# Expert gates added into a zeroed DRAM array by indirect transfers instead of routing matmuls

## The chip, the cores and the metric

One Trainium2 chip, one core. The time is device microseconds of one execution; where several were made, their median.

## The reference

One layer of a decoder, 512 tokens of 2048 numbers, all in float32. What comes ahead (projections, convolution branch, differential attention, first layer norm) is not touched. The change lies in the layer of experts ("peer"), for each block of tokens:

```python
q = (xb @ w_q).reshape(TOKEN_BLOCK, PEER_HEADS, 2, PEER_HALF)
s = jnp.einsum('thcd,hcnd->thcn', q, sub_keys).astype(jnp.float32)
vals, idx = lax.top_k(s, PEER_TOPK)
cand = vals[:, :, 0, :, None] + vals[:, :, 1, None, :]
cand_ids = idx[:, :, 0, :, None] * PEER_N_KEYS + idx[:, :, 1, None, :]
best, pos = lax.top_k(cand.reshape(TOKEN_BLOCK, PEER_HEADS, PEER_TOPK * PEER_TOPK), PEER_TOPK)
...
g = jax.nn.softmax(best, axis=-1)
h = jax.nn.gelu(jnp.einsum('td,thkd->thk', xb, u_tab[ids]))
return jnp.einsum('thk,thkd->td', g * h, v_tab[ids])
```

Each token picks 8 x 16 = 128 of 128 x 128 = 16384 experts, each with a gate g. The expert's down row u gives one number h, and g * h weighs its row v.

## The kernel before

A matmul in float32 accuracy is made of three float32r passes (lines 631 to 633): the weights raw, loaded from ws in units of 1 MB (two blocks of 128 x 1024), are split into whi (ACT, line 1027) and wlo = raw - whi (POOL, line 594, or DVE, line 1611), the activations likewise into ahi and alo. one_block issues 24 matmuls. Loads are issued by SP (load_unit, line 415), each as soon as the wlo of the unit two earlier is done.

Stages: projections and heads (B1), branches (B2), output projection and residual (B3, the result is res, kept in SBUF), the experts' queries and key scores (B4), then two long stages: up-projection of all 16384 experts (256 blocks from B5; 64 expert_steps of 4), and value stage (256 blocks from B6). For the first TU = 352 tokens both are done densely: all experts, 352 columns. The remaining 160 tokens go sparsely: POOL gathers the picked rows (gather_rows, line 614: an indirect DMA of 128 rows of 8 KB), and DVE multiplies and sums each with the token (dot, line 1623, a scalar_tensor_tensor of 128 x 2048). 32 of the tokens (x1e, extra_dot) are spread over 128 partitions, 32 gathers; the last 128 take 128 gathers: NUP = 160 in all, with RING = 4 in flight. DVE names the next row (line 1617) when a buffer is free, and then does its other work in program order: lo_part, dot, and in some blocks one-hots.

For the dense tokens the up-projection gives gelu(x u) of every expert, which ACT writes from PSUM to DRAM (gelu_spill, [128 units, 128, 384]). The value stage needs it times the gate of (expert, token), zero where a token did not pick the expert. This array of gates is built by matmul, while the up-projection runs: for each token, PE multiplies two one-hot matrices,

```python
mm = pe.matmul(ps_g[s][:, k * P:(k + 1) * P], hot1[:, s, k], hot2w[:, s, k],
               start=True, stop=True)
```

hot1[pick, i1] and hot2w[pick, i2] times the gate, contracted over the token's 128 picks. 384 tokens (352 and the 32 extra ones, whose "gate" is g * h and whose gelu is set to 1) are done 4 at a time: DVE makes the one-hots (one_hots, line 1600), ACT scales them (scale_hots, line 1204), PE multiplies (route, line 875), ACT copies the result to gst (take_group, line 1211). A tile is RT = 64 tokens in 32 blocks; the first 16 blocks carry a group each. SP stores gst (4 MB) to route_spill per tile (line 500), six tiles in all. gst has the place of res, so res is stored before (spill_x1, line 475) and loaded back at the end of the up-projection (line 532). In the value stage load_hg loads gelu and gates for two units, and DVE multiplies them (expert_weights, line 1698).

Before the first tile PE transposes the picks (turn_picks, line 865) and DVE copies them from PSUM (line 1590).

The order of POOL in this stretch: the subtractions of the first 40 blocks of the up-projection, spread_picks, then 160 gathers and 128 gathers of v rows, with nothing between. From block 40 (DVE_LO) on, DVE subtracts.

## Time and profile before

| | |
|---|---|
| median of 3 runs | 3902.03 us (3900.24 to 3908.92) |
| the profiled execution | 3903.89 us, span 3902.1 us |
| PE matmul busy | 3808.9 us, 98% |
| DVE busy | 2682.2 us, 69% |
| ACT busy | 1403.7 us, 36% |
| POOL busy | 1265.6 us, 32% |
| read from HBM, written | 788.21 MB, 67.11 MB |

PE is TensorE's matmul queue, PEld its weight loads, DVE VectorE, ACT ScalarE, POOL GpSimd, SP the queue that issues most loads. The view of lines gives a group's busy time and the mean of one; the timeline gives each instruction's start and length and, in brackets, the idle time before it and what ended it; windows add up busy time between two points. Busy time of PE counts overlapping matmuls once, so it says that the engine has work, not that it runs at its peak. For gathers POOL's time is that of issuing, and the landing is listed apart.

### The profile page before, as it was taken

The page shows a single profiled execution, that of the slowest core. Times are in us where ns is not written, and L with a number is a line of the kernel's source. Part 1 is how long each engine was busy: PE and PEld are TensorE (multiplying, and loading weights), DVE is VectorE, ACT ScalarE, POOL GpSimd, SP SyncE. Part 2 cuts the span into 40 slices and gives each one's busy share as a digit, 9 for nine tenths or more (in the row PEclk, how much of TensorE's full clock was granted, in tenths as well). Part 3 has the DMA queues.
Part 4 walks back from the last instruction along what each step waited for, and adds up shares of the span by engine and source line. Part 5 has one row for each costly group of instructions (what it writes and reads, how often), then busy time and mean ns, then how long its engine had stood idle before and what let it go on. Part 6 is the DMA issues. An engine that isn't in the chain of part 4 may idle for free.

```text
span 3902.1 us, 57973 instructions
## 1 busy us (share of the span) xinstructions
PE 3808.9 (98%) x20449; PEld 3471.3 (89%) x20449; DVE 2682.2 (69%) x3814; ACT 1403.7 (36%) x1992; POOL 1265.6 (32%) x620
## 2 busy tenths in 40 slices
PE   8999999999998999999999999989999999999999
PEld 6888888878886889999999999989999999999777
DVE  3555555534413899878878878778888888898642
ACT  4433444441114223446546545222222222222442
POOL 4444444434443447422222222212212211222233
PEclk9999999999999999999999999999999999999999
DMA  4222222224433324698998898978877877787332
GB/s 156 95 97 97 102 94 94 94 99 152 148 121 108 108 89 160 232 367 321 361 373 314 340 378 328 404 294 315 306 288 279 318 289 283 285 311 278 119 105 78
DMA packets 210825, 856.40 MB, mean 219 GB/s; under 512 B 17520, under 2 KB 107824, under 8 KB 119216
## 3 DMA queue, kind: packets, MB, share of 16 engines
q1 hardware_dynamic: 137648, 515.62, 36.6%
q0 software_dynamic: 41600, 302.04, 19.2%
q10 hardware_dynamic: 31488, 37.76, 2.7%
q8 instruction: 30, 0.49, 0.1%
q14 instruction: 59, 0.48, 0.0%
HBM read 788.21 MB, written 67.11 MB: 219 GB/s over the span
## 4 chain that ended last, share of the span: by engine, by line
PE 75%; DVE 9%; DMA 7%; DVEq 3%; ACT 3%; issue 2%; ACTq 1%; SPq 0%
PE bank L631 24%; PE bank L633 23%; PE bank L632 23%; DMA raw<-ws 7%; DVE wlo L1611 2%; PE bank L875 2%; DVEq L1625 2%; DVE yacc L1715 2%; ACT whi L1027 1%; DVE sc L1416 1%; PE bank L674 1%; DVEq L1709 1%; PE bank L693 1%; DVE hot L1600 1%; DVE res L1757 1%
## 5 line engine op out<-in xcount | busy, mean ns | idle before, releaser
L1027 ACT ACTIVATE whi<-raw 128x1024 fp32r<-128x1024 f32 x784 | 820.6, 1057 | 2253.9 <-PE bank L633 1429.2
L631 PE MATMUL bank<-ahi,whi 128*128 128x352 f32 (+1 forms) x3968 | 1434.6, 362 | 32.2 <-DVE alo L1365 7.9
L632 PE MATMUL bank<-alo,whi 128*128 128x352 f32 (+1 forms) x3968 | 1413.8, 356 | 0.0
L633 PE MATMUL bank<-ahi,wlo 128*128 128x352 f32 (+1 forms) x3968 | 1413.6, 356 | 0.0
L594 POOL TENSOR_TENSOR wlo<-raw,whi 128x1024 fp32r<-128x1024 f32 x316 | 792.0, 2510 | 1050.3 <-ACT whi L1027 1021.5
L631 PEld LDWEIGHTS bank<-ahi,whi 128*128 128x128 f32 x3968 | 749.8, 189 | 126.7 <-issue 35.9
L633 PEld LDWEIGHTS bank<-ahi,wlo 128*128 128x128 f32 x3968 | 749.4, 189 | 77.3
L632 PEld LDWEIGHTS bank<-alo,whi 128*128 128x128 f32 x3968 | 749.5, 189 | 72.1 <-issue 0.5
L1611 DVE TENSOR_TENSOR wlo<-raw,whi 128x1024 fp32r<-128x1024 f32 x472 | 574.7, 1223 | 190.6 <-ACT whi L1027 188.3
L631 PE MATMUL bank<-xwhi,whi 128*128 128x384 f32 x2048 | 686.7, 335 | 19.3 <-ACT hst L1226 10.3
L633 PE MATMUL bank<-xwhi,wlo 128*128 128x384 f32 x2048 | 685.7, 335 | 0.0
L632 PE MATMUL bank<-xwlo,whi 128*128 128x384 f32 x2048 | 685.6, 335 | 0.0
L614 POOL DMA_INDIRECT vrows<-v_tab,idxs x128 | 218.3, 1705 | 878.1 <-DVE idxs L1617 868.3
L614 POOL DMA_INDIRECT urows<-u_tab,idxs x160 | 250.7, 1567 | 673.3 <-DVE idxs L1617 663.3
L631 PEld LDWEIGHTS bank<-xwhi,whi 128*128 128x128 f32 x2048 | 385.7, 188 | 21.7 <-issue 21.4
L632 PEld LDWEIGHTS bank<-xwlo,whi 128*128 128x128 f32 x2048 | 385.7, 188 | 0.0
L633 PEld LDWEIGHTS bank<-xwhi,wlo 128*128 128x128 f32 x2048 | 385.6, 188 | 0.0
L1715 DVE SCALAR_TENSOR_TENSOR yacc<-vrows,hd,yacc 128x2048 f32<-128x2048 f32 x127 | 298.7, 2352 | 23.4 <-issue 20.6
L1623 DVE SCALAR_TENSOR_TENSOR urows<-urows,x1n 128x2048 f32<-128x2048 f32 x128 | 292.5, 2285 | 0.0
L1416 DVE SCALAR_TENSOR_TENSOR sc<-glu,cur,sc 128x512 f32<-128x512 f32 x232 | 270.1, 1164 | 17.3
L1204 ACT ACTIVATE hot2w<-hot,gT 128x128 f32<-128x128 f32 x384 | 122.9, 391 | 116.6 <-DVE hot L1600 116.6
L1382 DVE RECIPROCAL rcp<-sums 128x2 f32<-128x2 f32 x32 | 5.3, 166 | 231.1 <-ACTq L1085 231.1
(218 smaller groups left out, 2809.8 us busy)
## 6 DMA issues: line engine op xcount, KB each, us to landing
raw<-ws SPq DMA_DIRECT2D x394, 1024.0 KB, 4.9
gelu_spill<-hst ACTq DMA_DIRECT2D x128, 192.0 KB, 3.7
route_spill<-gst SPq DMA_DIRECT2D x24, 1024.0 KB, 14.8
hg<-gelu_spill SPq DMA_DIRECT2D x64, 384.0 KB, 6.7
hg<-route_spill SPq DMA_DIRECT2D x64, 384.0 KB, 7.4
gate_spill<-gout ACTq DMA_DIRECT2D x32, 256.0 KB, 2.1
gl<-gate_spill SPq DMA_DIRECT2D x32, 256.0 KB, 2.7
xin<-xT SPq DMA_DIRECT2D x8, 512.0 KB, 8.6
```

Of the source, the lines that this page charges most:

```text
L594: nc.gpsimd.tensor_tensor(wlo[:, s], raw[:, s // 2, s % 2], whi[:, s].bitcast(F32), ALU.subtract).then_inc(lo_done, 1)
L614: nc.gpsimd.indirect_dma_start(rows[:, s], None, table, bass.IndirectOffsetOnAxis(ap=idxs[:, s, 0:1], axis=0)).then_inc(rows_in[s], 16)
L631: pe.matmul(ps_out, hi, xh, start=first, stop=False)
L632: pe.matmul(ps_out, hi, xl, start=False, stop=False)
L633: return pe.matmul(ps_out, lo, xh, start=False, stop=last)
L875: mm = pe.matmul(ps_g[s][:, k * P:(k + 1) * P], hot1[:, s, k], hot2w[:, s, k], start=True, stop=True)
L1027: act.activation(whi[:, s], raw[:, s // 2, s % 2], ACT.Copy).then_inc(hi_done, 1)
L1204: sc2 = act.activation(hot2w[:, s, k], hot2[:, s, k], ACT.Copy, scale=gT[:, bass.ds(4 * g + k, 1)])
L1416: dve.scalar_tensor_tensor(dst, glu[:, w:w + T], cur[:, w:w + 1], acc, ALU.mult, ALU.add)
L1611: dve.tensor_tensor(wlo[:, s], raw[:, s // 2, s % 2], whi[:, s].bitcast(F32), ALU.subtract).then_inc(lo_done, 1)
L1623: dve.scalar_tensor_tensor(rows, rows, 1.0, x1n[:, :, TD:T], ALU.mult, ALU.mult, accum_out=hd[:, bass.ds(n, 1)])
L1715: dve.scalar_tensor_tensor(yacc[:], vrows[:, s], w, yacc[:], ALU.mult, ALU.add)
```

## The change

- The gates' array is half of a new DRAM array, expert_spill [128 units, 128, 2, 384]: [.., 0, :] is gelu, [.., 1, :] the gates. SP fills the gates' half with zeros during the first stage: 32 transfers of 4 x 128 x 384 numbers from a tile of zeros, one after every two weight loads.
- DVE works out for each of 3 token blocks and 128 picks the flat place of the gate (goff) and keeps the gates (gval).
- POOL adds each pick's column of 128 gates (one per token) to DRAM with an indirect DMA, `compute_op=ALU.add`, 4 bytes per token: 384 such transfers (put_gate). Those of the first two token blocks come behind gathers 0 to 99 (EARLY), alternating between the blocks in sixteens, those of the third behind gathers 100 to 149 (LATE), after the 32 extra tokens' values have been brought into gval (extra_gates). Every 16 puts of a block POOL waits until the block's earlier ones have landed.
- turn_picks, route, one_hots, scale_hots, take_group, both stores and loads of res and the table, and gst are gone. res stays in SBUF.
- load_hg is one transfer for gelu and gates. The first two come behind load k = 6 of the last 12 (before: k = 2 and 4), when all puts have landed.
- TILE_DOTS: a dot in three of every four blocks, instead of 11 in the first 16 and 13 in the last 16.

```diff
@@ -85,12 +83,15 @@
 NXP = NP // NJ
 NUP = NXP + NP
 NTG = 24
-TILE_DOTS = [j % 2 == 1 or j in (4, 8, 12) if j < 16 else j not in (18, 23, 28) for j in range(32)]
+TILE_DOTS = [j % 4 != 3 for j in range(32)]
 POST_DOTS = [j % 5 != 4 and j < 20 for j in range(4 * (64 - POST))]
 assert sum(TILE_DOTS) == NTG and NTG * NRT + sum(POST_DOTS) == NUP and NTG % RING == 0
 assert NTG < NXP <= 2 * NTG
+EARLY = [(NUP - 60) * j // (2 * NP) for j in range(2 * NP)]
+LATE = [NUP - 60 + 50 * j // NP for j in range(NP)]
 LEAD = 2
...
-    gelu_sp = nc.dram_tensor("gelu_spill", (NK, P, TD), F32).ap()
-    route_sp = nc.dram_tensor("route_spill", (NRT, P, NK * RT), F32).ap()
+    eg_sp = nc.dram_tensor("expert_spill", (NK, P, 2, TD), F32).ap()
+    eg_flat = eg_sp.rearrange("k p c (t o) -> (k p c t) o", o=1)
...
+        hg = small("hg", [P, 2, 2, 2, TD])
+        wt = small("wt", [P, TD])
+        o_route_end = c[0]
...
-            with sp.Fori(0, (U1 + U1T) // 2) as i:
+            sp.wait_ge(const_ok, 1)
+            with sp.Fori(0, NK // 4) as i:
+                for s in range(2):
+                    load_unit(2 * i + s, s)
...
+                k4 = sp.snap(i * 4)
+                sp.dma_start(eg_sp[bass.ds(k4, 4), :, 1].rearrange("k p t -> p k t"),
+                             zero[:].unsqueeze(1).broadcast_to((P, 4, TD))).then_inc(zero_out, 16)
+            with sp.Fori(NK // 4, (U1 + U1T) // 2) as i:
...
-            def spill_x1(q):
-                sp.wait_ge(ln[1]["lo_ok"], 4 * q + 4)
-                sp.dma_start(x1_sp[:, 4 * q:4 * q + 4], res[:, 4 * q:4 * q + 4]).then_inc(x1_out, 16)
...
-                sp.wait_ge(g_evac, t * GT + (2 + GT))
-                for q in range(6):
-                    n = NK * RT // 4
-                    if q < 4:
-                        sp.dma_start(route_sp[tt, :, q * n:(q + 1) * n], gst[:, q * n:(q + 1) * n]
-                                     ).then_inc(tile_out, 16)
-                    load_unit(16 * t + (B5 // 2 + 2 * PRE + 10 + q), q % 2)
...
             def load_hg(k, s):
                 k2 = sp.snap(k * 2)
-                sp.dma_start(hg[:, s, 0].rearrange("p (c t) -> p c t", c=2),
-                             gelu_sp[bass.ds(k2, 2)].rearrange("c p t -> p c t")).then_inc(hg_in[s], 16)
-                kk = sp.snap(k * 2 * RT)
-                sp.dma_start(hg[:, s, 1].rearrange("p (a x) -> p a x", a=NRT),
-                             route_sp[:, :, bass.ds(kk, 2 * RT)].rearrange("a p x -> p a x")
+                sp.dma_start(hg[:, s], eg_sp[bass.ds(k2, 2)].rearrange("k p c t -> p k c t")
                              ).then_inc(hg_in[s], 16)
-            expert_loads(0, PRE)
-            with sp.Fori(0, NRT) as t:
-                tile_loads(t)
+            expert_loads(0, U4 // 2 + POST)
...
             for k in range(2 * (64 - POST)):
                 load_unit(B5 // 2 + 2 * POST + k, k % 2)
-                if k == 1:
-                    sp.wait_ge(tile_out, 64 * NRT)
-                    sp.wait_ge(g_full, TD // 4)
+                if k == 2:
+                    sp.dma_start(pin[:], pT).then_inc(p_in, 16)
+                if k == 6:
+                    for a in range(TD // P):
+                        sp.wait_ge(put[a], 16 * NP)
                     for s in range(2):
                         sp.wait_ge(gelu_out[s], 16 * 4)
-                    sp.dma_start(pin[:], pT).then_inc(p_in, 16)
-                if k in (2, 4):
-                    load_hg(k // 2 - 1, k // 2 - 1)
-                if k in (3, 5, 7, 11):
-                    q = (3, 5, 7, 11).index(k)
-                    sp.dma_start(res[:, 4 * q:4 * q + 4], x1_sp[:, 4 * q:4 * q + 4]).then_inc(x1_in, 16)
...
         def _(pool):
             nc.gpsimd.memset(ones[:], 1.0)
             nc.gpsimd.memset(eps[:], EPS)
+            nc.gpsimd.memset(zero[:], 0.0)
+            nc.gpsimd.iota(gcol[:], [[P, TD // P]], base=TD, channel_multiplier=1,
+                           allow_small_or_imprecise_dtypes=True)
             nc.gpsimd.memset(ident[:], 0.0)
...
-            def gather_rows(first, n_rows, table, rows):
+            def put_gate(a, n):
+                if n == 0:
+                    pool.wait_ge(offs_ok, 1)
+                    pool.wait_ge(zero_out, 16 * NK // 4)
+                if n % TOPK == 0 and n:
+                    pool.wait_ge(put[a], 16 * n)
+                nc.gpsimd.indirect_dma_start(
+                    eg_flat, bass.IndirectOffsetOnAxis(ap=goff[:, a, n:n + 1], axis=0),
+                    gval[:, a, n:n + 1], None, compute_op=ALU.add).then_inc(put[a], 16)
+            def extra_gates():
+                pool.wait_ge(hx_w, 1)
+                for j in range(NJ):
+                    pool.dma_start(gval[P - NX:P, TU // P, j * NXP:(j + 1) * NXP],
+                                   hx[j * NX:(j + 1) * NX]).then_inc(xw_in, 16)
+                pool.wait_ge(xw_in, 16 * NJ)
+            def put_gates(n):
+                for j, at_row in enumerate(EARLY):
+                    if at_row == n:
+                        put_gate(j // TOPK % 2, j // (2 * TOPK) * TOPK + j % TOPK)
+                if n == LATE[0]:
+                    extra_gates()
+                for j, at_row in enumerate(LATE):
+                    if at_row == n:
+                        put_gate(TU // P, j)
+            def gather_rows(first, n_rows, table, rows, gates=False):
                 for n in range(n_rows):
                     s = n % RING
@@ -614,10 +603,12 @@
                     nc.gpsimd.indirect_dma_start(
                         rows[:, s], None, table,
                         bass.IndirectOffsetOnAxis(ap=idxs[:, s, 0:1], axis=0)).then_inc(rows_in[s], 16)
+                    if gates:
+                        put_gates(n)
             lo_parts(0, DVE_LO)
             spread_picks()
-            gather_rows(0, NUP, u_tab, urows)
+            gather_rows(0, NUP, u_tab, urows, gates=True)
             gather_rows(NUP, NP, v_tab, vrows)
...
-            def turn_picks():
...
-            def route(g, s):
-                pe.wait_ge(hot_scaled, g + 1)
-                pe.wait_ge(g_evac, g + 1)
-                for k in range(4):
-                    mm = pe.matmul(ps_g[s][:, k * P:(k + 1) * P], hot1[:, s, k], hot2w[:, s, k],
-                                   start=True, stop=True)
-                mm.then_inc(g_full, 1)
...
-            pe.wait_ge(sc_free, U4 + 2)
-            pe.wait_ge(x1e_ok, 5)
-            turn_picks()
-            with pe.Fori(0, NRT) as t:
-                t = pe.snap(t)
-                with pe.Fori(0, 4) as i:
-                    expert_step(8 * t + i + PRE, GT * t + 4 * i)
-                with pe.Fori(4, 8) as i:
-                    expert_step(8 * t + i + PRE)
-            with pe.Fori(POST, 64) as i:
+            with pe.Fori(1, 64) as i:
...
-            def scale_hots(g, s):
...
-            def take_group(t, g, s):
-                act.wait_ge(g_full, GT * t + g + 1)
-                act.activation(gst[:].rearrange("p (k t) -> p t k", t=RT)[:, bass.ds(4 * g, 4), :],
-                               ps_g[s][:].rearrange("p (t k) -> p t k", t=4), ACT.Copy).then_inc(g_evac, 1)
...
+                        act.dma_start(eg_sp[i * 2 + u, :, 0], hst[:, u]).then_inc(gelu_out[u], 16)
...
-            expert_step(PRE - 1)
-            routing_tile(0, first=True)
-            routing_tile(1)
+            with act.Fori(PRE - 1, PRE + 16) as i:
+                expert_step(i)
             act.wait_ge(hx_ok, 1)
             act.activation(hx[:], hx[:], ACT.Gelu_apprx_tanh).then_inc(hx_gelu, 1)
-            with act.Fori(2, NRT) as t:
-                routing_tile(act.snap(t))
-            with act.Fori(POST, 64) as i:
+            with act.Fori(PRE + 16, 64) as i:
                 expert_step(i)
...
+            dense = slice(0, TD // P)
+            dve.scalar_tensor_tensor(gflat[:].rearrange("p a n -> p (a n)"),
+                                     i2n[:, dense].rearrange("p a h k -> p (a h k)"), float(NK),
+                                     i1n[:, dense].rearrange("p a h k -> p (a h k)"), ALU.mult, ALU.add)
+            dve.tensor_copy(gval[:].rearrange("p a n -> p (a n)"),
+                            gn[:, dense].rearrange("p a h k -> p (a h k)"))
             dve.drain()
...
-                dve.wait_ge(g_full, GT * t + (g - 1))
+            for a in range(TD // P):
+                dve.tensor_scalar(gflat[:, a], gflat[:, a], 2.0 * TD, gcol[:, a:a + 1], ALU.mult, ALU.add)
+            dve.drain()
+            dve.tensor_copy(goff[:].rearrange("p a n -> p (a n)"), gflat[:].rearrange("p a n -> p (a n)"))
+            dve.drain().then_inc(offs_ok, 1)
...
                 for j, with_dot in enumerate(TILE_DOTS):
                     lo_part(32 * t + (DVE_LO + LEAD + j), (j + LEAD) % 4)
-                    if j < GT:
-                        if j >= 2 or not first:
-                            hots_free(t, j)
-                        one_hots(t, j)
                     if with_dot:
                         next_dot()
...
+            expert_tile(0, extra=True)
+            expert_tile(1, extra=True)
+            expert_tile(2)
             dve.wait_ge(hx_gelu, 1)
-            dve.tensor_tensor(hx[:], hx[:], xg[:, 1], ALU.mult)
-            dve.drain()
-            dve.transpose(gT[:, TU:TD], hx[:])
-            dve.drain()
-            routing_tile(NRT - 1)
+            dve.tensor_tensor(hx[:], hx[:], xg[:, 1], ALU.mult).then_inc(hx_w, 1)
+            with dve.Fori(3, NRT) as t:
+                expert_tile(t)
...
-                dve.wait_ge(hg_in[s], g * 64 + 32 * (k // 4 + 1))
-                dve.tensor_tensor(wt[:].rearrange("p (a t) -> p a t", a=NRT),
-                                  hg[:, s, 0, (k % 2) * TD:(k % 2 + 1) * TD].rearrange("p (a t) -> p a t", a=NRT),
-                                  hg[:, s, 1].rearrange("p (a c t) -> p c a t", a=NRT, c=2)[:, k % 2], ALU.mult)
+                dve.wait_ge(hg_in[s], g * 32 + 16 * (k // 4 + 1))
+                dve.tensor_tensor(wt[:], hg[:, s, k % 2, 0], hg[:, s, k % 2, 1], ALU.mult)
```

On POOL, where the gathers begin, before: the end of the loop of subtractions, the transfers of the picks, then all gathers (urows, vrows are their buffers; a wait stands at the instruction that carries it, xN counts equal ones).

```order
L598 REGISTER_ALU
L598 COMPARE_AND_BRANCH
L606 DMA xg<-xsrc 32x2x32 [waits xsrc_ok]
L606 DMA xg<-xsrc 32x2x32 x3
L614 DMA urows<-u_tab,idxs 128x2048 [waits idx_ok] x160
L614 DMA vrows<-v_tab,idxs 128x2048 [waits idx_ok] x128
```

And in the changed kernel in the late part, from gather 103 or so (expert_spill<-gval is a put):

```order
L575 DMA expert_spill<-gval,goff 12582912x1 x2
L603 DMA urows<-u_tab,idxs 128x2048 [waits idx_ok]
L575 DMA expert_spill<-gval,goff 12582912x1 x3
L603 DMA urows<-u_tab,idxs 128x2048 [waits idx_ok]
L575 DMA expert_spill<-gval,goff 12582912x1 [waits put2]
L575 DMA expert_spill<-gval,goff 12582912x1
L603 DMA urows<-u_tab,idxs 128x2048 [waits idx_ok]
L575 DMA expert_spill<-gval,goff 12582912x1 x3
```

Two or three puts stand now behind each gather up to number 149, and a put that waits for put2 is ahead of the next gather.

On DVE, in a block of the looped tile, before (wlo is the subtraction, hot_149 and hot_155 are the one-hots hot1 and hot2, urows,hd the dot; ISA and REGISTER_ALU set registers):

```order
L1611 TENSOR_TENSOR wlo<-raw,whi 128x1024 [waits hi_done]
L1606 ISA
L1600 ISA [waits g_full]
L1600 TENSOR_TENSOR hot_149<-i1T,iota 128x512
L1600 REGISTER_ALU
L1600 TENSOR_TENSOR hot_155<-i2T,iota 128x512
L1610 REGISTER_ALU
L1611 TENSOR_TENSOR wlo<-raw,whi 128x1024 [waits hi_done]
L1600 ISA [waits g_full]
L1600 TENSOR_TENSOR hot_149<-i1T,iota 128x512
L1600 REGISTER_ALU
```

and now:

```order
L1526 REGISTER_ALU [waits rows_in1]
L1526 SCALAR_TENSOR_TENSOR urows,hd<-urows,x1n 128x2048
L1520 ISA
L1520 COPY idxs<-idx 128x1
L1513 REGISTER_ALU
L1514 TENSOR_TENSOR wlo<-raw,whi 128x1024 [waits hi_done]
L1513 REGISTER_ALU
L1514 TENSOR_TENSOR wlo<-raw,whi 128x1024 [waits hi_done]
L1526 REGISTER_ALU [waits rows_in2]
L1526 SCALAR_TENSOR_TENSOR urows,hd<-urows,x1n 128x2048
```

The one-hots and their wait for g_full are gone; subtraction and dot follow each other, and behind a dot that waits for its row (rows_in) stands the next block's subtraction.

## Rows read from the trace of the kernel before

**Rows 1.** The page: span, busy time of each engine, and 40 slices (tenths busy)

```profile
span 3902.1 us, 57973 instructions
PE 3808.9 (98%) x20449; PEld 3471.3 (89%) x20449; DVE 2682.2 (69%) x3814; ACT 1403.7 (36%) x1992; POOL 1265.6 (32%) x620
PE   8999999999998999999999999989999999999999
DMA  4222222224433324698998898978877877787332
```

**Rows 2.** The chain of work that ended last, by line (page)

```profile
PE bank L631 24%; PE bank L633 23%; PE bank L632 23%; DMA raw<-ws 7%; DVE wlo L1611 2%; PE bank L875 2%; DVEq L1625 2%; DVE yacc L1715 2%; ACT whi L1027 1%; DVE sc L1416 1%; PE bank L674 1%; DVEq L1709 1%; PE bank L693 1%; DVE hot L1600 1%; DVE res L1757 1%
```

**Rows 3.** Windows: busy us of PE, PEld, DVE, ACT, POOL; clock, DMA, GB/s

```profile
1609.90:2477.80 867.90, 851.58 (x5467) 842.05 (x5468) 698.91 (x834) 451.48 (x772) 237.64 (x150) 0.99 0.90 348
2477.80:2530.00 52.20, 48.92 (x293) 47.97 (x292) 34.63 (x39) 13.48 (x17) 13.06 (x10) 0.97 1.02 413
```

**Rows 4.** Timeline of POOL before the routing begins: start us, us, what

```profile
1573.40 2.70 POOL L594 TENSOR_TENSOR wlo<-raw,whi 128x1024 fp32r<-128x1024 f32 x1 [0.66 <-ACT whi L1027]
...
1588.86 2.70 POOL L594 TENSOR_TENSOR wlo<-raw,whi 128x1024 fp32r<-128x1024 f32 x1 [0.65 <-ACT whi L1027]
```

**Rows 5.** The first window for line 875 alone: PE, PEld; clock, DMA, GB/s

```profile
1609.90:2477.80 867.90, 105.58 (x768) 97.11 (x768) 0.99 0.90 348
```

**Rows 6.** Timeline of DVE: one subtraction and one dot without one-hots

```profile
2114.16 1.23 DVE L1611 TENSOR_TENSOR wlo<-raw,whi 128x1024 fp32r<-128x1024 f32 x1
2115.30 2.29 DVE L1623 SCALAR_TENSOR_TENSOR urows<-urows,x1n 128x2048 f32<-128x2048 f32 x1
2118.00 1.23 DVE L1611 TENSOR_TENSOR wlo<-raw,whi 128x1024 fp32r<-128x1024 f32 x1
```

**Rows 7.** Timeline of POOL, a gather behind a subtraction and one behind nothing

```profile
1737.51 1.68 POOL L614 DMA_INDIRECT urows<-u_tab,idxs  x1 [5.71 <-DVE idxs L1617]
1741.08 0.94 POOL L614 DMA_INDIRECT urows<-u_tab,idxs  x1 [1.90 <-DVE idxs L1617]
```

**Rows 8.** Timeline of DVE in the same stretch

```profile
1734.72 2.29 DVE L1633 SCALAR_TENSOR_TENSOR urows<-urows,x1e 128x2048 f32<-128x2048 f32 x1
1737.16 1.22 DVE L1611 TENSOR_TENSOR wlo<-raw,whi 128x1024 fp32r<-128x1024 f32 x1
1738.29 2.29 DVE L1633 SCALAR_TENSOR_TENSOR urows<-urows,x1e 128x2048 f32<-128x2048 f32 x1
```

**Rows 9.** Timeline of DVE, then of POOL, early in the value stage

```profile
2611.20 2.35 DVE L1715 SCALAR_TENSOR_TENSOR yacc<-vrows,hd,yacc 128x2048 f32<-128x2048 f32 x1
2611.36 3.00 POOL L614 DMA_INDIRECT vrows<-v_tab,idxs  x1 [31.87 <-DVE idxs L1617]
2614.66 1.05 POOL L614 DMA_INDIRECT vrows<-v_tab,idxs  x1 [0.30 <-issue]
```

**Rows 10.** DMA issues, median us to landing (page, and the DMA view)

```profile
raw<-ws SPq DMA_DIRECT2D x394, 1024.0 KB, 4.9
urows<-u_tab,idxs POOLq DMA_INDIRECT x160, 9.3
xg<-xsrc POOLq DMA_DIRECT2D x4, 8.0 KB, 1.7
```

**Rows 11.** DMA queues: packets, MB, share of 16 engines' span

```profile
q0 software_dynamic: 41600, 302.04, 19.2%
q10 hardware_dynamic: 31488, 37.76, 2.7%
```

**Rows 12.** Who waited for whom around the first routed step, and around the stage's end

```profile
DVE gT L1590 <- PE bank L865: 5.0, 1, 5.0
PE bank L631 <- DVE wlo L1611: 3.1, 1, 3.1
...
ACT whi L1027 <- DMA raw<-ws: 59.3, 10, 14.9
PE bank L631 <- ACT hst L1226: 13.7, 4, 10.3
```

127 lines of the change are left out of this document (22 added, 105 removed).

## The prediction

> **What bounds the kernel now.** I read the page first: TensorE (PE) is busy 3808.9 of 3902.1 us, and the slices show 9 tenths or more nearly throughout [rows 1]. The chain of work that ended last agrees: 70% of it is the three f32 matmul lines 631 to 633, 7% is weight loads from DRAM (raw<-ws), and the routing matmuls of line 875 are 2% [rows 2]. So a PE instruction taken away is worth its time, as long as no other engine then sets the pace. The change works in one stage, the up-projection of the 16384 experts (256 blocks). I cut out the stretch from gather 0 to gather 150, 1609.9 to 2477.8 us: 867.9 us, PE busy 851.6, DVE 698.9, POOL 237.6 in 150 gathers, DMA engines 0.90 busy [rows 3]. That is 5.79 us a gather, or 17.4 us for three gathers and the four blocks that belong to them.
>
> What would PE need alone? Before the routing begins, POOL's subtractions of equal position are 15.46 us apart over four blocks [rows 4]: 3.865 us a block. The 150 gathers span 200 blocks (24 per 32), so 773 us. The missing 95 us are the routing: its 384 matmuls (768 records) are busy 105.6 us in this stretch [rows 5], part of it under the blocks' own.
>
> **The sum, part by part.**
>
> *Removed from PE:* 384 routing matmuls and 9 transposes. Worth 95 us in the stretch, if nothing else binds.
>
> *Removed from DVE and ACT:* the one-hots, scalings and copies of line 1600, 1204 and 1211. DVE now needs for a subtraction and a dot 3.84 us start to start [rows 6], for a subtraction alone 1.2 us: four subtractions and three dots are 3 x 3.84 + 1.2 = 12.7 us per four blocks, under PE's 15.46. DVE alone doesn't bind. ACT has even less to do.
>
> *Removed from SP's queue:* 24 MB of stores and as many bytes of loads of the routing table, and 4 MB out and 4 MB in of the residual. Around the stage's end ACT waits 59.3 us for weights in 10 waits, which share the queue with residual and table loads, and PE waits once 10.3 us [rows 12]. Gather 149 is issued behind dot 145, in the second of the stage's last 24 blocks; from there to the value stage it takes 95 us for some 22 blocks that need 85. I give back 10 us.
>
> *At the first routed step:* DVE waits 5.0 us for the turned picks and PE 3.1 us for DVE [rows 12]. Both waits and the transposes go; six short DVE operations on up to 384 columns, which name the places of the puts, take theirs. Worth 6 us. The rest of PE's stall is the picks' own chain and stays.
>
> *Moved to the first stage:* 32 zero fills of 768 KB on SP, one per two weight units. The DMA engines are 20 to 40% busy there [rows 1], and a weight load lands in 4.9 us [rows 10] and has the time of two blocks, 7.7 us at least. I cost it at nothing, hidden behind PE's matmuls; without that cover 512 packets at the 0.0535 us worked out in rival 2 are 1.7 us a fill, 55 us.
>
> *Added to POOL:* 384 indirect adds ("puts"), 128 elements of 4 bytes each, 256 of them after gathers 0 to 99, 128 after 100 to 149: 2.56 per gather throughout. No row shows an indirect store with an addition. The nearest are the gathers, which are also one indirect instruction over 128 partitions. A gather behind nothing takes 0.94 us, one behind a subtraction 1.68 us [rows 7], and the DVE rows beside them say why: the subtraction runs 1737.16 to 1738.38, the gather ends 0.81 us later at 1739.19 [rows 7, 8]. Early in the value stage a gather starts 0.16 us into a 2.35 us accumulation and takes 3.00 us, ending 0.81 us after it; the next one starts 0.30 us later [rows 9]. So an indirect instruction that comes upon a DVE operation with two SBUF inputs waits for its end, then needs 0.81 us; a put costs POOL between 0.94 + 0.30 = 1.24 us and 3.3 us. I take the gather's own behaviour. Where DVE's operations follow one another, POOL gets through one per operation: 7 in the 12.7 us. What is left of the 3 + 7.68 = 10.68 instructions per four blocks, 3.68, goes at 1.24 us, 4.6 us. That is 17.3 us per four blocks against PE's 15.46: **POOL becomes the bound**, DVE waits for its rows, and the subtractions queued behind the dots on DVE, which PE waits for, are late with them. 50 x 17.3 = 865 us, against 867.9 before. The saving on PE is used up.
>
> *Added waits on POOL:* every 16 puts of one token block it waits until the earlier ones have landed. For the 256 early puts the two blocks alternate, so these landed 16 puts ago: nothing. The last 128 are of one block; 7 waits are for the put just issued, with the next gather queued behind them. A landing is between 1.7 us (8 KB) and 9.3 us (a gather) [rows 10]; a put is small but stands behind a gather in the same queue, so I take 5: 35 us, bounds 12 and 65. The late gates' own transfers (four, 1.7 us to landing) add 5. Since POOL has no slack in this case, all 40 count.
>
> The Trainium skill ("DMA: Bandwidth & Descriptors", Anatomy of one DMA) gives some 2.0 us of fixed cost to a DMA issued by GpSimd; by it the 7 waits would be 14 us and the time about 3902 us. No row here shows a small indirect transfer; its value lies within my bounds.
>
> *The sum:* 865 + 40 = 905 us instead of 868, +37; -6 and -10: +21 us. The profiled execution took 3903.9 us beside its span of 3902.1, so 3925; it lies 1.9 us over the median of the three runs: **3923 us**. With the bounds of the waits this case runs from 3895 to 3950. Chance 0.33.
>
> **The rivals.**
>
> *1. POOL keeps up (faster).* If a put costs near 1.24 us because it finds DVE in a pause, 150 gathers and 384 puts are 534 x 1.24 = 662 us, under PE's 773. The stretch falls by 95 and the waits disappear in the four rows of lead (four gathers are in flight, 20 us): -95 - 6 - 10 = -111, 3791 us. It decides on the other side from about 1.45 us a put in the mean. For it: DVE does pause 2.8 us per four blocks. Against: a gather averages 1.58 us (237.6 / 150) [rows 3], and that is without two or three puts behind it. Full: 0.20. Halfway, some 3850 us: 0.17.
>
> *2. The DMA engines become the bound.* In the stretch they are busy 0.90 x 867.9 = 781 us. An 8 KB packet costs 0.192 x 3902 x 16 / 41600 = 0.288 us, so the 24 stores of the table were 24 x 8 x 0.288 = 55 us of each engine: 726 without them. The puts are 49,152 packets. The cheapest data packets that the queue rows show are 1.2 KB ones at 0.0535 us (0.027 x 3902 x 16 / 31488) [rows 11]: 164 us of each engine, 890 us in all, just under POOL's 905 and so hidden by it. If a put has to read its place in DRAM and write it, at that price twice, it is 1054 us: +186 - 16, 4074 us. It decides from 905 us on, 0.058 us a packet. For it: the share was 1.02 right after the stretch [rows 3], so the engines do run full. Against: 4 bytes are less than 1.2 KB. 0.12.
>
> *3. A put is more work than a gather.* At 1.1 us instead of 0.94 a put no longer fits between the starts of a subtraction and a dot (1.14 us apart [rows 6]), with its 0.30 us: POOL passes about 4 instead of 7 in DVE's 12.7 us, and the other 6.7 take 1.4 each: 22.1 us per four blocks, 1105 us, +237 + 40 - 16: 4165 us. Nothing in the trace excludes that an addition takes more descriptor work. 0.14.
>
> *4. POOL holds DVE up too.* Then each instruction would add its 0.81 us to DVE: 12.7 + 10.68 x 0.81 = 21.4 us per four blocks, 1070 us, with waits 4130 us. The rows speak against it: the dot at 1738.29 ran beside the working part of a gather and took 2.29 us, like the one at 1734.72 beside none [rows 8]. 0.03. The Trainium skill ("SBUF — State Buffer", SBUF: two separate sides) calls the port pair of DVE and GpSimd an exclusive lock that blocks whichever comes second; the trace agrees for POOL behind DVE and not for DVE behind POOL.
>
> *5. The change doesn't do what it says* (PE's matmuls gone, same time because the stage was loaded by DMA anyway): 0.01; PE is 98% busy in the stretch.
>
> **How the numbers follow.** About 0.2% is what a measurement of this kernel can tell from no change, 8 us. Faster: rival 1 whole and half, and the low edge of the forecast, 0.20 + 0.17 + 0.03 = 0.40. Same: the forecast's part from 3894 to 3910 and the last rival, 0.08. Slower: the rest of the forecast and rivals 2 to 4, 0.52. The range runs from rival 1 in full, 3790, to past rival 2, 4110; rivals 3 and 4 above it are left out (0.17). Cases of both signs are likely; the forecast's own range is 3895 to 3950.
>
> **What would show it.** Right: in the stage POOL is busy all the time and the idle time before its gathers is gone; DVE's dots wait for gathers, not for ACT; the 150 gathers take about 905 us; puts last 0.94 to 3 us; in the second part there are 7 gaps on POOL of some 5 us; PE is idle some 15% of the stretch. PE and clock in the other stages are unchanged, and no load waits behind a zero fill. Wrong: blocks 3.87 us apart in the stage and POOL with pauses (rival 1); DMA share at 1.0 with weights late (rival 2); puts of over 1.1 us with DVE idle (rival 3); dots longer than 2.29 us (rival 4).

## The result and the profile after

The changed kernel takes 4150.15 us (median of 4 runs, 4145.11 to 4159.1) beside 3901.51 us for the kernel before in the same session: ratio 1.0636, 95% interval 1.061 to 1.0661, so 6.4% slower. The forecast of 3923 us had the right sign and the right engine as the new bound, and lay 227 us too low; the measured time is above the range, which ended at 4110.

The page after, with the lines that answer to [rows 1, 2]:

```profile
span 4143.3 us, 55256 instructions
PE 3817.7 (92%) x19672; PEld 3466.9 (84%) x19672; DVE 2568.3 (62%) x3624; ACT 1230.4 (30%) x1545; POOL 1989.0 (48%) x1010
PE   8999999999999998777887777779999999999989
POOL 4444444334543467888888888851112121212233
PE 59%; POOL 23%; DVE 8%; issue 5%; DMA 2%; DVEq 2%; ACT 1%; ACTq 0%; SPq 0%; POOLq 0%
PE bank L622 19%; PE bank L624 19%; PE bank L623 19%; POOL expert_spill L575 18%; POOL urows L603 5%; DVE hot L1461 1%; DMA expert_spill<-gval,goff 1%; DMA raw<-ws 1%; PE bank L665 1%; DVE sc L1324 1%; PE bank L684 1%; DVE pick L1464 0%; DV
L622 PE MATMUL bank<-ahi,whi 128*128 128x352 f32 (+1 forms) x3968 | 1475.1, 372 | 293.9 <-DVE wlo L1514 260.6
L575 POOL DMA_INDIRECT expert_spill<-gval,goff x384 | 761.2, 1982 | 133.3 <-issue 114.6
L603 POOL DMA_INDIRECT urows<-u_tab,idxs x160 | 214.1, 1338 | 65.0 <-issue 46.6
L1526 DVE SCALAR_TENSOR_TENSOR urows<-urows,x1n 128x2048 f32<-128x2048 f32 x128 | 293.4, 2292 | 415.2 <-DMA urows<-u_tab,idxs 415.0
```

PE is no longer busy throughout: for some twelve slices it is at 7 or 8 tenths, and in most of those POOL is at 8. POOL, absent from the chain before, has 23% of it. The puts take 1982 ns each. DVE waits 415 us for rows, PE waits 261 us for DVE's subtractions, and dots still last 2292 ns.

Windows of the changed kernel, gather 0 to gather 150 and the value stage (columns as in [rows 3]):

```profile
1606.90:2748.80 1141.90, 883.00 (x4821) 858.55 (x4822) 596.21 (x650) 282.71 (x335) 962.88 (x538) 0.89 0.79 248
2825.20:3892.30 1067.10, 1067.08 (x6144) 1066.70 (x6144) 921.92 (x1140) 270.49 (x256) 221.32 (x131) 1.00 0.77 297
```

The granted clock is 0.89 in the long stretch, where PE stands still for 259 of 1142 us, against 0.99 before. Where the 241 us between the two profiled spans are:

| stretch | before | after | difference |
|---|---|---|---|
| start to gather 0 | 1609.9 | 1606.9 | -3 |
| gather 0 to gather 150 | 867.9 | 1141.9 | +274 |
| gather 150 to the value stage | 94.8 | 76.4 | -18 |
| value stage | 1079.6 | 1067.1 | -12.5 |
| rest | 249.9 | 251.0 | +1 |

The long stretch is POOL's. Waits of POOL in it:

```profile
POOL expert_spill L575 <- issue: 114.6, 376, 0.3
POOL urows L603 <- issue: 45.4, 149, 0.3
POOL expert_spill L575 <- DMA expert_spill<-gval,goff: 15.0, 7, 3.9
POOL expert_spill L575 <- DMA gval<-hx: 3.7, 1, 3.7
```

Added up: puts 761, gathers 200, 0.30 us between any two 160, landings 19: 1140 of 1142 us. POOL does nothing else there and, but for 1.6 us at the start, waits for no engine's signal, so neither the lower clock nor anything else on PE adds to the time of this stretch. Its timeline shows what a put is:

```profile
2009.65 1.55 POOL L575 DMA_INDIRECT expert_spill<-gval,goff  x1 [0.30 <-issue]
2011.51 1.55 POOL L575 DMA_INDIRECT expert_spill<-gval,goff  x1 [0.30 <-issue]
2019.25 1.00 POOL L603 DMA_INDIRECT urows<-u_tab,idxs  x1 [0.30 <-issue]
2025.63 3.44 POOL L575 DMA_INDIRECT expert_spill<-gval,goff  x1 [0.31 <-issue]
```

and DVE's beside it:

```profile
2006.68 1.21 DVE L1514 TENSOR_TENSOR wlo<-raw,whi 128x1024 fp32r<-128x1024 f32 x1
2011.98 2.29 DVE L1526 SCALAR_TENSOR_TENSOR urows<-urows,x1n 128x2048 f32<-128x2048 f32 x1 [4.09 <-DMA urows<-u_tab,idxs]
2025.36 2.29 DVE L1526 SCALAR_TENSOR_TENSOR urows<-urows,x1n 128x2048 f32<-128x2048 f32 x1 [1.97 <-DMA urows<-u_tab,idxs]
```

A gather with nothing in its way takes 1.00 us here (0.94 in [rows 7]); a put with nothing in its way takes 1.55 us. One that begins inside a dot (2025.63, dot to 2027.65) ends 1.42 us behind it at 2029.07, where a gather needed 0.81. The put of 2011.51 began 0.47 us ahead of its dot and neither was held up. So 384 x (1.55 + 0.30) + 150 x 1.30 = 905 us of POOL are needed even with DVE out of the way, more than PE's 773.

### The profile page after: what moved, and what is told of

It reads as the page before. It is cut to its first block, busy times and chain, and to the rows that moved or that the text cites. A ratio compares the mean times of both kernels' runs of the same rounds, so it can differ in the third digit from the quotient of the medians.

```text
span 4143.3 us, 55256 instructions
## 1 busy us (share of the span) xinstructions
PE 3817.7 (92%) x19672; PEld 3466.9 (84%) x19672; DVE 2568.3 (62%) x3624; ACT 1230.4 (30%) x1545; POOL 1989.0 (48%) x1010
## 3 DMA queue, kind: packets, MB, share of 16 engines
q0 software_dynamic: 97024, 302.28, 21.9%
## 4 chain that ended last, share of the span: by engine, by line
PE 59%; POOL 23%; DVE 8%; issue 5%; DMA 2%; DVEq 2%; ACT 1%; ACTq 0%; SPq 0%; POOLq 0%
PE bank L622 19%; PE bank L624 19%; PE bank L623 19%; POOL expert_spill L575 18%; POOL urows L603 5%; DVE hot L1461 1%; DMA expert_spill<-gval,goff 1%; DMA raw<-ws 1%; PE bank L665 1%; DVE sc L1324 1%; PE bank L684 1%; DVE pick L1464 0%; DVE topi L1425 0%; DVE topi L1418 0%; DVE s4b L1419 0%
## 5 line engine op out<-in xcount | busy, mean ns | idle before, releaser
L622 PE MATMUL bank<-ahi,whi 128*128 128x352 f32 (+1 forms) x3968 | 1475.1, 372 | 293.9 <-DVE wlo L1514 260.6
L623 PE MATMUL bank<-alo,whi 128*128 128x352 f32 (+1 forms) x3968 | 1449.8, 365 | 0.0
L624 PE MATMUL bank<-ahi,wlo 128*128 128x352 f32 (+1 forms) x3968 | 1447.1, 365 | 0.0
L622 PEld LDWEIGHTS bank<-ahi,whi 128*128 128x128 f32 x3968 | 779.8, 197 | 412.0 <-DVE wlo L1514 290.3
L624 PEld LDWEIGHTS bank<-ahi,wlo 128*128 128x128 f32 x3968 | 779.4, 196 | 77.4
L623 PEld LDWEIGHTS bank<-alo,whi 128*128 128x128 f32 x3968 | 780.7, 197 | 72.1 <-issue 0.5
L575 POOL DMA_INDIRECT expert_spill<-gval,goff x384 | 761.2, 1982 | 133.3 <-issue 114.6
L1514 DVE TENSOR_TENSOR wlo<-raw,whi 128x1024 fp32r<-128x1024 f32 x472 | 570.2, 1221 | 27.7 <-ACT whi L984 24.6
L1526 DVE SCALAR_TENSOR_TENSOR urows<-urows,x1n 128x2048 f32<-128x2048 f32 x128 | 293.4, 2292 | 415.2 <-DMA urows<-u_tab,idxs 415.0
L603 POOL DMA_INDIRECT urows<-u_tab,idxs x160 | 214.1, 1338 | 65.0 <-issue 46.6
```

Of the source, the lines that this page charges most:

```text
L575: nc.gpsimd.indirect_dma_start(eg_flat, bass.IndirectOffsetOnAxis(ap=goff[:, a, n:n + 1], axis=0), gval[:, a, n:n + 1], None, compute_op=A ...
L603: nc.gpsimd.indirect_dma_start(rows[:, s], None, table, bass.IndirectOffsetOnAxis(ap=idxs[:, s, 0:1], axis=0)).then_inc(rows_in[s], 16)
L622: pe.matmul(ps_out, hi, xh, start=first, stop=False)
L623: pe.matmul(ps_out, hi, xl, start=False, stop=False)
L624: return pe.matmul(ps_out, lo, xh, start=False, stop=last)
L1514: dve.tensor_tensor(wlo[:, s], raw[:, s // 2, s % 2], whi[:, s].bitcast(F32), ALU.subtract).then_inc(lo_done, 1)
```

## Experiments

**My theory after the result** was that POOL's work per put sets the time, most of it the addition's, the rest waits behind DVE. The rivals: DMA traffic or landings, and DVE's dots alone.

### All puts left out

```diff
-                if n % TOPK == 0 and n:
-                    pool.wait_ge(put[a], 16 * n)
-                nc.gpsimd.indirect_dma_start(
-                    eg_flat, ...)
+                pass
```

(SP's wait for the landed puts, ahead of the value stage's first load, is left out with them.)

> The changed kernel without its 384 indirect adds (the gates stay zero, so the dense experts add nothing); zero fills, offsets and the joined load stay. Theory 'POOL sets the pace by the puts': the stretch from gather 0 to gather 150 falls from 1142 us to PE's 773, so about 4143 - 369 = 3774 us, ratio to the kernel before 0.967. Rival 'the DMA engines or the zero fills cost it': less than half of the loss goes, over 3950 us.

Measured: 3769.01 us, ratio 0.9654 (0.9638 to 0.967). The same stretch, 1606.9 to gather 150:

```profile
1606.90:2360.90 754.00, 752.26 (x4666) 751.47 (x4667) 584.77 (x640) 281.88 (x326) 236.95 (x155) 1.00 0.94 369
```

The puts and their waits account for 381 us (4150 - 3769). All else in the change is worth 134 us of gain, and PE alone needs 754 us, not 773. The DMA engines are 0.94 busy here and 0.79 with the puts: they follow, they don't bound. The zero fills are in this run too and land in 7.9 us; the up-projection begins at the same time as before.

### The addition taken away

```diff
-                    gval[:, a, n:n + 1], None, compute_op=ALU.add).then_inc(put[a], 16)
+                    gval[:, a, n:n + 1], None).then_inc(put[a], 16)
```

> The 384 puts as plain indirect stores, without the addition (where two heads pick the same expert one gate is lost). Theory 'the addition makes a put dearer than a gather': the shortest put falls from 1.55 us to about 0.94 us, and the stretch to some 870 to 905 us, 3870 to 3910 us in all. Rival 'any indirect store of 4 bytes costs 1.55 us on POOL': time as with the addition, 4140 to 4150 us, shortest put 1.55 us.

Measured: 3975.45 us, ratio 1.018 (1.0163 to 1.0197); the stretch is 967 us. Both lie above what the theory said (905 and 3910 at most), though the shortest put did fall as it said. The puts' group and three of them on POOL:

```profile
L575 POOL DMA_INDIRECT expert_spill<-gval,goff x384 | 570.0, 1484 | 151.5 <-issue 114.6
```

```profile
1999.61 0.99 POOL L575 DMA_INDIRECT expert_spill<-gval,goff  x1 [0.30 <-issue]
2000.91 2.61 POOL L575 DMA_INDIRECT expert_spill<-gval,goff  x1 [0.30 <-issue]
2009.90 0.97 POOL L575 DMA_INDIRECT expert_spill<-gval,goff  x1 [0.30 <-issue]
```

A plain indirect store costs what a gather costs, 0.97 us. The addition alone is 0.58 us an instruction and 175 us of the stretch (1142 - 967). 384 x 0.58 would be 223; of these some 18 come back in shorter landings, and some 31 because fewer instructions begin inside a DVE operation of over 1 us (220 of the 534, against 290 here).

The queue of the indirect transfers, without puts and with plain ones:

```profile
q0 software_dynamic: 41728, 302.06, 19.6%
q0 software_dynamic: 54016, 302.28, 20.1%
```

The full kernel has 97,024 packets in it. So a plain put makes (54016 - 41728) / 384 = 32 packets and an adding one (97024 - 41728) / 384 = 144. POOL's time does not follow their number: a gather makes 144 as well (41600 / 288) [rows 11] and takes 1.0 us. That leaves the addition as the cause; what POOL does longer for it is not shown.

### Half and a quarter of the puts

```diff
+                if n % 2:
+                    return
                 nc.gpsimd.indirect_dma_start(
```

(for the quarter `n % 4`; the waits count accordingly)

> Every second put left out, 192 stay, in the same places (half of the gates missing). Theory 'POOL sets the pace, and only once it has no slack': 192 x 2.28 + 150 x 1.64 = 684 us of POOL's time lie under PE's 773, so 3775 to 3800 us. Rival 'each put costs its own time wherever it stands' (packets, or PE held up): half of the 369 us stays, about 3960 us.

> Every fourth put stays, 96 in all (three quarters of the gates missing). Theory 'POOL with slack': as without puts, 3774 to 3780 us. Rival 'each put costs its own time': a quarter of the 369 us stays, about 3866 us.

Measured: 192 puts 3795.81 us (3781.8 to 3805.78), ratio 0.9732 (0.9716 to 0.9749); 96 puts 3769.18 us, ratio 0.9657 (0.9641 to 0.9673). Their groups:

```profile
L577 POOL DMA_INDIRECT expert_spill<-gval,goff x192 | 384.7, 2004 | 88.4 <-issue 56.1
```

```profile
L577 POOL DMA_INDIRECT expert_spill<-gval,goff x96 | 218.8, 2280 | 44.5 <-issue 27.4
```

Each put takes as long as in the full kernel or longer, and yet 96 cost nothing, 192 cost 27 us and 384 cost 381. This is what a second engine does below and above its capacity: with 192 puts the stretch is 772 us, just over PE's 754. A cost that each put adds wherever it stands would have grown in proportion. The window with 192 puts:

```profile
1607.00:2379.30 772.30, 764.81 (x4747) 762.74 (x4748) 592.33 (x646) 282.00 (x329) 634.10 (x346) 1.00 1.01 362
```

Two engines are full in it. POOL is busy for 634 us, and but for the 0.30 us between instructions and the landings it waits only 7 us: it is at the end of its capacity, where the expectation had left it 89 us of slack, because a gather takes 1.65 + 0.30 us here and not 1.64 with its pause. The DMA engines' share is 1.01. Which of the two costs these few us is not separated. A put with nothing in its way takes 1.55 to 1.58 us here too, so a full DMA does not lengthen it.

### Dots of one number

```diff
-                dve.scalar_tensor_tensor(rows, rows, 1.0, x1n[:, :, TD:T], ALU.mult, ALU.mult,
-                                         accum_out=hd[:, bass.ds(n, 1)])
+                dve.tensor_copy(hd[:, bass.ds(n, 1)], rows[:, 0, 0:1])
```

(and the same for the dots of the extra tokens)

> The changed kernel with its 160 dots on DVE replaced by a copy of one number per partition (the sparse tokens' values are wrong), same order and waits. Theory 'a put waits behind a DVE operation with two SBUF inputs': without the dots only subtractions are in the way, puts average 1.6 to 1.7 us instead of 1.98, the stretch is some 940 to 990 us and the time 3940 to 3990 us. Rival 'the put's length is its own work alone': 1142 us stay, 4140 to 4150 us.

Measured: 4012.55 us, ratio 1.028 (1.0265 to 1.0295); stretch 1006 us, somewhat over what was expected; puts 1671 ns, gathers 1139. With the dots gone 136 us come back, and 1006 are left where 905 are bare instructions: the subtractions still hold POOL up, and 33 us are landings. So neither the dots nor the addition alone turn the change into a gain.

### Half the partitions

```diff
-                    eg_flat, bass.IndirectOffsetOnAxis(ap=goff[:, a, n:n + 1], axis=0),
-                    gval[:, a, n:n + 1], None, compute_op=ALU.add).then_inc(put[a], 16)
+                    eg_flat, bass.IndirectOffsetOnAxis(ap=goff[0:64, a, n:n + 1], axis=0),
+                    gval[0:64, a, n:n + 1], None, compute_op=ALU.add).then_inc(put[a], 16)
```

> All 384 puts, each for 64 partitions instead of 128 (half of the tokens get no gates). Theory 'a put's time on POOL goes with its elements': the shortest put falls from 1.55 us to about 1.0 us, time about 3900 to 3950 us. Rival 'a put's time is per instruction': 1.55 us, 4140 us.

Measured: 4110.11 us, ratio 1.0528 (1.0513 to 1.0543). Neither theory is met; the result is nearer to the one by instruction. The shortest put takes 1.39 us instead of 1.55, for half the elements: an estimate from these two is 1.24 us per instruction and 2.4 ns per element. Fewer tokens per put would not help; fewer puts would.

### Runs of 512 bytes in the value stage

The value stage is 12.5 us shorter than before. The first idea was the load of the gates, now one run per partition and unit instead of six pieces. Here they are read in 512-byte pieces by a DMA of their own, from another array of the right size (DVE's wait and its operands follow, not shown):

```diff
-                sp.dma_start(hg[:, s], eg_sp[bass.ds(k2, 2)].rearrange("k p c t -> p k c t")
-                             ).then_inc(hg_in[s], 16)
+                sp.dma_start(hg[:, s, 0], eg_sp[bass.ds(k2, 2), :, 0].rearrange("k p t -> p k t")
+                             ).then_inc(hg_in[s], 16)
+                kk = sp.snap(k * 128)
+                sp.dma_start(hg[:, s, 1].rearrange("p c t -> p (c t)").rearrange("p (a x) -> p a x", a=6),
+                             u_tab[0:24 * P].rearrange("(a p r) d -> a p (r d)", a=6, p=P)[:, :, bass.ds(kk, 128)]
+                             .rearrange("a p x -> p a x")).then_inc(hg_in[s], 16)
```

> The changed kernel, but gelu and gates are loaded apart in the value stage, and the gates' half in six runs of 512 bytes per partition as before (read from another array of the same shape, so the gates are wrong). Theory 'the value stage became 12 us shorter because its loads have longer runs and weights wait less': it goes back from 1067 to about 1080 us, 4162 us in all. Rival 'it comes from the residual that stays in place, or from the state in which the stage is entered': stays at 1067 us, 4150 us.

Measured: 4154.58 us, value stage 1067.4 us. ACT waited 249 us for weights in it instead of 151, and PE not at all. The theory fell.

### A hybrid: a third of the gates put

Since 96 to 192 puts cost little, the kernel before was given 128 puts (tokens 0 to 127, behind gathers 0 to 95) and routes the other 256 tokens by matmul, four tiles instead of six. The whole computation is done.

```diff
-            with pe.Fori(0, NRT) as t:
+            with pe.Fori(PRE, PRE + 8 * T0) as i:
+                expert_step(i)
+            with pe.Fori(0, NRT - T0) as t:
...
+                        for j, at_row in enumerate(PUTS):
+                            if at_row == n:
+                                put_gate(j)
```

> The kernel before, with the gates of tokens 0 to 127 put by 128 indirect adds behind gathers 0 to 95 and the other 256 tokens routed by matmuls in the last four of six tiles; all is computed. Theory 'POOL has slack for some 190 puts': the 32 routing groups taken from PE are worth about 1 us each, 3870 us, ratio 0.992. Rival 'a put costs its own time wherever it stands': 128 x 0.96 us more than that, about 3990 us.

Measured: 3910.89 us, ratio 1.0018 (1.001 to 1.0027). The value stage begins 16 us earlier (2556.2 us) and takes 1101.9 us, 22 more. Then the third load per pair of units was merged into the first:

> The version of the run before this one (the kernel before, with the gates of tokens 0 to 127 put by 128 indirect additions and the other 256 tokens routed by matmul), but the put gates stand behind the gelu numbers in one array of 512 columns, so that a load of two units is again two transfers (1024 numbers and 512 numbers per partition) and not three. Nothing of the computation is left out. Theory A, the 22 us that the value stage lost to 1101.9 us came from the third transfer among the loads of weights: the value stage is back at 1080 us, the time near 3889 us, about 0.3% under the kernel before. Theory B, they came from the second multiplication of DVE or from the 128 more gate columns' bytes, which are still there: value stage near 1100 us and the time near 3908 us, the same as the kernel before. PE's and POOL's part up to the value stage is expected unchanged in both, start of the value stage near 2556 us.

Measured: 3908.09 us, ratio 1.0016 (1.0007 to 1.0025), value stage 1100.1 us: theory B's numbers, so the third load was not the cause.

### The place of a loop in the code

The timeline of DVE in the kernel before, where the value stage's loop jumps back (once in some 135 us):

```profile
2846.79 1.23 DVE L1611 TENSOR_TENSOR wlo<-raw,whi 128x1024 fp32r<-128x1024 f32 x1
2855.09 0.56 DVE L1698 TENSOR_TENSOR wt<-hg 128x384 f32<-128x384 f32 x1 [7.07 <-issue]
```

and in the changed kernel:

```profile
3100.93 0.56 DVE L1593 TENSOR_TENSOR wt<-hg 128x384 f32<-128x384 f32 x1 [1.96 <-issue]
```

The same instruction waits for nothing that the profile shows, 7 us in one and 2 in the other. The loop body is 303 instructions of DVE in both, but stands at another place in its program. Two runs moved it by empty instructions in a pause of DVE: 98 in the kernel before, away from the place with the long pause, and 158 in the changed one, onto it:

```diff
+            for _ in range(98):
+                dve.drain()
             head(0, first=True)
```

> The kernel before with 98 empty instructions (drains) on DVE ahead of its first attention head, where it waits 18.6 us for PE, so that every later loop of DVE stands 98 instructions further on in its program; nothing of the computation is left out. In the traces the value stage's loop is 303 instructions of DVE in the kernel before and in the changed one, but begins at instruction 1586 in the former and 1428 in the latter, and DVE stands idle 7.07 us at its head in the former and 1.96 us in the latter, once per iteration; PE then waits 1.1 to 2.4 us each time. Theory A, the place of the loop in DVE's code sets that pause (1586 + 98 and 1428 are 256 apart): pauses of 2 us at the loop's head, value stage near 1068 us, time near 3890 us. Theory B, the pause comes from the multiplication that stands at the loop's head (its operands or its wait for the loaded gates) or a shift of another size would be needed: pauses stay at 7 us, value stage 1080 us, time 3902 us.

> The changed kernel with 158 empty instructions (drains) at the same place, so that the value stage's loop begins at instruction 1586 of DVE as in the kernel before; nothing of the computation is left out. Theory A, the place in the code: the pause at the loop's head grows from 2 to 7 us and the value stage from 1067 to about 1079 us, time near 4162 us. Theory B, the instruction at the loop's head: pause 2 us, value stage 1067 us, time near 4150 us.

Measured: the kernel before so shifted takes 3892.82 us, ratio 0.9976 (0.9967 to 0.9985), its value stage 1068.8 us. The changed kernel takes 4148.48 us (2 runs), its value stage 1073.6 us instead of 1067.1; its total hides this, since the stage begins 5 us earlier (2820.1 us). The pauses, in the first and in the second:

```profile
2849.59 0.56 DVE L1700 TENSOR_TENSOR wt<-hg 128x384 f32<-128x384 f32 x1 [1.94 <-issue]
```

```profile
3100.49 0.56 DVE L1595 TENSOR_TENSOR wt<-hg 128x384 f32<-128x384 f32 x1 [7.17 <-issue]
```

The pause goes and comes with the place of the loop. In the changed kernel it came in full but cost 6.5 us, not the 12 of theory A: PE then stood still 1.1 us in five iterations, and 1.1 to 2.4 us in the kernel before. So the place of the loop is shown as a cause of 10.8 us in one direction and of 6.5 in the other, and between 2 and 6 us of the 12.5 stay open.

The hybrid was then rebuilt with the kernel before's own multiplication (303 instructions) and 12 empty ones:

> The hybrid again (gates of tokens 0 to 127 by 128 puts behind gathers 0 to 95, tokens 128 to 383 routed by matmul), with the put gates behind the gelu numbers of each pair of units, in the order of the routing table, so that a load is two transfers and the multiplication is the kernel before's own single instruction; the value stage's loop is then 303 instructions of DVE as in the kernel before, and 12 empty ones ahead of the first head set it at instruction 1684, where the run before this pair had 2 us pauses. Nothing of the computation is left out. Theory A, puts cost nothing up to one per gather or so and the value stage's time depends on the place of its loop in DVE's code alone: value stage begins near 2554 us, takes 1068 us, time 3875 us, 0.7% under the kernel before. Theory B, the hybrid's loads or layout cost the value stage something of their own: value stage 1090 us or more, time 3895 us or above. Theory C, in between, if the loop is right but the two-transfer load with more bytes keeps ACT waiting for weights: 1075 us, 3882 us.

Measured: 3906.95 us, ratio 1.0007 (0.9998 to 1.0016), value stage 1096.9 us. These are theory B's numbers, but the trace points to another cause than loads or layout. The pause had moved to the third instruction behind the loop's head:

```profile
2842.94 0.56 DVE L1762 TENSOR_TENSOR wt<-hg 128x384 f32<-128x384 f32 x1 [2.18 <-issue]
2843.58 0.36 DVE L1766 CAST xwhi<-wt 128x384 fp32r<-128x384 f32 x1
2848.54 0.56 DVE L1768 TENSOR_TENSOR xwlo<-wt,xwhi 128x384 fp32r<-128x384 f32 x1 [4.61 <-issue]
```

and PE's weight loads pause too, twice in most iterations, released by nothing:

```profile
2837.65 0.19 PEld L671 LDWEIGHTS bank<-xwhi,whi 128*128 128x128 f32 x1 [2.30 <-issue]
2841.69 0.19 PEld L672 LDWEIGHTS bank<-xwlo,whi 128*128 128x128 f32 x1 [1.31 <-issue]
```

Three more runs shifted DVE by 16 further instructions, and PE by 0, 54 and 150:

```diff
             pe.matmul(ps_x[:, 0:2], ones[0:64, :], lamp[:], start=True, stop=True).then_inc(lam_sum, 1)
+            for _ in range(54):
+                pe.drain()
```

> The combined hybrid with 28 instead of 12 empty instructions on DVE, nothing of the computation left out. In the run before DVE's pause of 4.7 us stood a few instructions behind the head of the value stage's loop, not at it. Theory A (the code is fetched in pieces, a border close behind the place that a loop jumps back to costs 5 us, and 16 instructions more put the head beyond it): DVE's pause in the loop is 2 us, PE's gaps that follow it go, the value stage falls from 1097 by 6 to 12 us, time 3893 to 3900 us. Theory B (a pause that comes with the hybrid's code wherever it stands): value stage 1097 us, 3907 us.

> As the run before it, and 54 empty instructions on PE behind its first small matmul, where it waits 7.5 us. PE too shows pauses in the combined hybrid that no other engine ended (41.7 us in 23 waits of matmuls and weight loads, against one of 5 to 11 us in the kernels before and after), two in each iteration of the value stage's loop. Theory A, PE's own code is fetched in pieces as well and the place of its loop decides: this shift, or the one of the next run, takes the pauses of PE away, value stage 1070 to 1085 us, time 3875 to 3890 us. Theory B: no change against the run before.

> As the run before it with 150 empty instructions on PE instead of 54: the shift by which the loop would stand as in the kernel before if a matmul were one instruction of PE's code (256 less the 106 by which the hybrid's loop begins later), where 54 is the one if it were two. Theory A: one of the two has a value stage of 1070 to 1085 us and the other not. Theory B: both are like the first of the three.

Measured: 3909.09 us, **3877.86 us** and 3886.78 us; ratios 1.0013 (1.0003 to 1.0022), 0.9942 (0.9925 to 0.9959) and 0.9955 (0.9938 to 0.9971). With DVE alone shifted, DVE's pause at the loop is gone and PE's remain: 1098.7 us, nothing gained where theory A had 6 to 12 us, so PE's own pauses were what counted. With PE shifted they are gone. (The 41.7 us of the expectation add up the waits of matmuls and of weight loads, which are mostly the same pauses.) The value stage with DVE alone shifted, then windows of the middle run, from about gather 0 to the value stage, and the value stage:

```profile
2553.55:3652.24 1098.70, 1077.70 (x6143) 1074.33 (x6144) 926.01 (x1139) 270.44 (x256) 226.08 (x131) 0.99 0.76 289
```

```profile
1609.00:2552.40 943.40, 907.89 (x5696) 900.70 (x5697) 727.29 (x850) 404.69 (x645) 519.53 (x288) 0.98 0.93 347
2552.40:3620.70 1068.30, 1067.64 (x6144) 1067.00 (x6144) 923.62 (x1140) 270.25 (x256) 226.12 (x131) 1.00 0.78 296
```

Of the 30.4 us between the two value stages, PE is idle for 20 (21.0 us against 0.7), and its busy time is 10 us longer, at a granted clock of 0.99 instead of 1.00. The last run has 1068.8 us, so both shifts of PE work and the distance between bad places was not found. It begins its value stage 16 us later than the middle run: it is 5.6 us behind at gather 0, and in the stretch after it PE stands idle some 7 us more, behind DVE's subtractions and ACT's scalings; why, was not followed.

The middle run beats both kernels: 0.6% under the kernel before, 6.6% under the changed one, with the whole computation. A third of the routing as puts gives some 20 us (2572.6 to 2552.4) and the code's place 11; what follows the value stage takes 4 us more than before, so the spans differ by 27.7 us. Against the kernel before at a good place of its own (3892.82 us) the gain is 15 us, 0.4%.

## Why the prediction came out as it did

**What bounds the kernel; PE alone 773 us.** Right in kind. Without puts the stretch is 754 us, so the removal was worth 114 us there, not 95: PE alone was priced 19 us too high, which changes nothing here, since PE isn't the bound.

**"I take the gather's own behaviour."** This is the step that failed, and it is a term mis-sized. A put alone takes 1.55 us instead of 0.94, ends 1.4 us behind a DVE operation instead of 0.81, and averages 1.98. Rows of a transfer in the other direction, without arithmetic, had been the nearest; they were right for the plain store (0.97) and wrong for the addition. The pair of bounds, 1.24 and 3.3 us with the pause, did hold the mean of 2.28, but not the single put: the one shown above takes 3.44 + 0.31 us. The addition costs 175 us (967 to 1142).

**"POOL gets through one per operation", 865 us.** The run with plain stores is the forecast's own world, and took 967 us with 37 of landings: 930 instead of 865. Its trace says where the 65 us are. 290 of the 534 instructions begin inside a DVE operation of over 1 us. That is fewer than the forecast's 7 x 50 = 350, but each loses 0.84 us by it, where the forecast had 12.7 / 7 - 1.24 = 0.57: 243 us instead of some 200. And an instruction with nothing in its way takes 0.98 us and not 0.94, 21 us in all. So it was the price of such a meeting that was too low, and not the number of meetings.

**Landing waits, 35 + 5 us.** Measured 15.0 + 3.7, with seven waits as foretold, 2.1 us each in the mean and 3.9 at most. The Trainium skill ("DMA: Bandwidth & Descriptors", Anatomy of one DMA) gives about 2.0 us of fixed cost to a DMA issued by GpSimd, nearly constant. The mean of these rows agrees. With plain stores the same seven waits took 30.9 us, 4.4 each, so here it is no constant. The whole: 237 us over the forecast's 905 are 65 for the passing, -3 for the landings in the run with plain stores (37 for 40), and 175 for the addition, in which 18 us of shorter landings are already taken off.

**First routed step -6, stage's end -10, zero fills 0.** Measured -3 and -18, and the fills cost nothing. Right within 8 us.

**"The other stages are unchanged."** The value stage lost 12.5 us. Moving DVE's loop in the code took 10.8 us from it in the kernel before and added 6.5 in the changed one; the change moved the loop by leaving code out ahead of it. What the rest is, stays open.

**The rivals.** Rival 3, a put as more work than a gather, is what happened: its time was 4165 us, 15 from the result, and it had a chance of 0.14. Its sign, puts of over 1.1 us with DVE idle, is there by far. That its number came so near is in part luck: it took 1.4 us for a put with DVE idle, pause included, where 1.85 are needed, and 40 us of landings where there were 19, and left the value stage unchanged. I had ranked it low because nothing in the rows spoke for it, but nothing spoke against it either, and the row on which the forecast stood showed no addition. Rival 1 (POOL keeps up) holds for 96 puts and nearly for 192. Rival 2 is out as the bound of this kernel: DMA share 0.79. Its price was near, though: 0.79 x 1142 = 902 us of the DMA engines in the stretch, beside its 890, and 0.81 x 967 = 783 with plain stores. An estimate from this: had the adding puts cost POOL no more than the forecast said, the DMA engines would have stood close to the bound. The indirect queue's share went from 19.2% [rows 11] to

```profile
q0 software_dynamic: 97024, 302.28, 21.9%
```

which is (0.219 x 4143 - 0.192 x 3902) x 16 / 55424 = 0.046 us for each packet more, if the others kept their time; the 0.0535 taken was near. Rival 4 is out: a dot beside a put takes 2.29 us. The Trainium skill ("SBUF — State Buffer", SBUF: two separate sides) would have whichever comes second blocked; these rows, as those before, show it for POOL alone.

**The signs.** POOL busy throughout and dots that wait for gathers came as said. The sizes did not: the 150 gathers take 1142 us and not 905, puts last up to 3.5 us and not 3, the seven gaps are 2.1 us and not 5, and PE is idle 23% of the stretch and not 15%.
